# Requesting the first sixteen value pages of the sample group's stick-breaking stage one stage earlier

## The reference, cut to what matters

```python
z = jnp.einsum('bqhd,blhd->bhql', q, k).astype(jnp.float32) * (D_HEAD ** -0.5)
log_beta = jax.nn.log_sigmoid(z)
log_keep = jnp.where(mask, log_beta - z, 0.0)
after = lax.cumsum(log_keep, axis=3, reverse=True) - log_keep
w = jnp.where(mask, jnp.exp(log_beta + after), 0.0)
return jnp.einsum('bhql,blhd->bqhd', w.astype(v.dtype), v)
```

## Time and profile before

| | us |
|---|---|
| median of 3 runs | 4935.95 |
| lowest and highest run | 4934.9, 4941.7 |
| span of the profiled execution, first to last instruction | 4937.4 |
| index stage's key requests by SP | 978.2 to 987.6 |
| stick-breaking stage, first instruction to last score cap | 988.6 to 1363.0 |

### The profile page before, as it was taken

One profiled execution on the slowest core, in us unless ns is written; L12 is line 12 of the kernel. 1 busy time (PEld: TensorE's weight loads), 2 busy tenths in 40 slices (PEclk: granted clock), 3 DMA queues, 4 the chain that ended last, 5 costly groups with the idle time before them and its releaser, 6 DMA issues. The chain is left out here.

```text
span 4937.4 us, 82552 instructions
## 1 busy us (share of the span) xinstructions
PE 4283.9 (87%) x33016; PEld 3158.5 (64%) x33016; DVE 2783.5 (56%) x3905; ACT 1081.8 (22%) x1979; POOL 319.0 (6%) x443
## 2 busy tenths in 40 slices
PE   8997989877767789999996999688886969999997
PEld 5565335444434478887993655377784548888896
DVE  4798665289921355555335122479986155555444
ACT  1200554344431112222001011122222012222100
POOL 0000000400054000000000000122220000000000
PEclk9998999899978899999997999799997979999998
DMA  3012000399965211112442231422213211111343
GB/s 101 22 39 64 1 1 1 89 345 348 363 192 155 70 34 42 42 42 59 118 118 90 70 111 65 156 62 56 62 34 154 73 63 39 40 42 52 103 116 119
DMA packets 539511, 463.29 MB, mean 94 GB/s; under 512 B 77602, under 2 KB 453962, under 8 KB 534747
## 3 DMA queue, kind: packets, MB, share of 16 engines
q1 hardware_dynamic: 508386, 409.36, 26.2%
q10 hardware_dynamic: 21088, 32.80, 2.0%
q0 software_dynamic: 9728, 16.80, 1.2%
HBM read 397.01 MB, written 61.71 MB: 93 GB/s over the span
## 5 line engine op out<-in xcount | busy, mean ns | idle before, releaser
L313 PE MATMUL proj_acc<-hT,oT 128*128 128x352 f32 x864 | 258.4, 462 | 6.2 <-SPq L287 6.2
L2440 PE MATMUL fdown_acc<-hidden,oT 128*128 128x176 f32 x1584 | 248.3, 316 | 0.0
L2440 PEld LDWEIGHTS fdown_acc<-hidden,oT 128*128 128x128 f32 x1584 | 242.8, 193 | 0.7 <-issue 0.5
L313 PEld LDWEIGHTS proj_acc<-hT,oT 128*128 128x128 f32 x864 | 165.4, 192 | 99.5 <-SPq L287 7.1
L2184 PE MATMUL fup_acc_a<-h,w_up_first 128*128 128x264 f32 x704 | 169.7, 396 | 50.8 <-ACTq L2217 50.8
L2184 PEld LDWEIGHTS fup_acc_a<-h,w_up_first 128*128 128x128 f32 x704 | 137.5, 196 | 77.4 <-ACTq L2217 52.9
L517 DVE TENSOR_SCALAR_CACHE_REDUCE oT<-scores,proj_cand 128x384 bf16<-128x384 f32 (+1 forms) x186 | 164.4, 943 | 1.1
L2184 PE MATMUL fup_acc_c<-h,oT 128*128 128x264 f32 x704 | 163.8, 386 | 0.0
L2184 PE MATMUL fup_acc_d<-oT 128*128 128x264 f32 x704 | 163.8, 386 | 0.0
L2184 PE MATMUL fup_acc_b<-oT 128*128 128x264 f32 x704 | 163.8, 386 | 0.0
L2184 PE MATMUL fup_acc_d<-h,oT 128*128 128x264 f32 x704 | 163.8, 386 | 0.0
(11 more groups left out here) (645 smaller groups left out, 8608.0 us busy)
## 6 DMA issues: line engine op xcount, KB each, us to landing
oT<-in_ffn_w_down SPq DMA_DIRECT2D x96, 704.0 KB, 4.5
fup_w<-in_ffn_w_up SPq DMA_DIRECT2D x66, 512.0 KB, 4.9
scores<-in_cache_sb_k SPq DMA_DIRECT2D x128, 256.0 KB, 5.8
qb<-in_cache_sb_k SPq DMA_DIRECT2D x128, 256.0 KB, 6.2
qi<-in_cache_sb_v SPq DMA_DIRECT2D x128, 256.0 KB, 5.8
ka<-in_cache_sb_v SPq DMA_DIRECT2D x128, 256.0 KB, 6.3
w_up_first<-in_ffn_w_up SPq DMA_DIRECT2D x22, 512.0 KB, 3.8
x_between<-oT SPq DMA_DIRECT2D x16, 528.0 KB, 2.7
```

Source lines behind the costliest of these rows:

```text
L313: last = pe.matmul(acc[u][0:m, c, 0:CW], w[u][:, k, 0:m], hT[:, k, c * CW:(c + 1) * CW], start=(k == 0), stop=(k == KD - 1))
L2440: last = pe.matmul(bank[n], weights[:, k, :], moving[:, k, :], start=begin and k == 0, stop=k == DOWN_K - 1, skip_group_check=True)
```

## The change

Value pages 0 to 15 are requested by SP in the index stage, right behind the sixteen key pages (`ask_step_values`), into the same ring slots as before. Their sixteen semaphores are therefore allocated before that stage. In the loop of the stick-breaking stage, iteration t no longer requests value page t but value page t + 8, from page 16 on; the wait of each request on the page it overwrites is unchanged.

```diff
+def step_value_slot(A, i):
+    return half_columns(A.qi, i) if i < STEP_PAGES // 2 else half_columns(A.ka, i - STEP_PAGES // 2)
+
+def ask_step_values(nc, eng, K, A, I, arrived):
+    vc = I.cache_sb_v[0].rearrange("n p h d -> n p (h d)")
+    for t0 in range(0, STEP_PAGES, 8):
+        numbers = page_numbers(nc, eng, K.pages_steps[0], 4 * NPG - 8 - t0, 8, vc.shape[0])
+        for i, number in enumerate(numbers):
+            eng.dma_start(step_value_slot(A, t0 + i), vc[bass.ds(number, 1)].rearrange("o p n -> p (o n)")).then_inc(arrived[t0 + i], 16)
...
-        k_in, next_in = K.step_keys_in, K.unit_keys_in
-        s.sems += k_in
-        v_in = [s.sem(f"v_in{i}") for i in range(VR)]
+        k_in, v_in, next_in = K.step_keys_in, K.step_values_in, K.unit_keys_in
+        s.sems += k_in + v_in
...
             for t in range(n_pages):
                 if t + KR < n_pages:
                     load_k(t + KR)
-                load_v(t)
+                if VR <= t + PP < n_pages:
+                    load_v(t + PP)
             ask_unit_keys(nc, sp, K, A, I, next_in)
...
             ask_step_keys(nc, sp, K, A, I, own, K.step_keys_in)
+            ask_step_values(nc, sp, K, A, I, K.step_values_in)
...
+            K.step_values_in = [nc.alloc_semaphore(f"step_values_in{i}") for i in range(STEP_PAGES)]
```

## The result

The changed kernel takes 5074.01 us (median of 4 runs, 5071.06 to 5081.21) against 4937.56 (4 runs, 4934.9 to 4941.7): 2.8% slower, ratio 1.0278 with a 95% interval of 1.0265 to 1.029. The forecast was 5008 with a range of 4975 to 5045. Sign and place were right, and the size was too small: 136 us instead of 72.

The account below looks back on a forecast made before the run. DVE's 11.20 us per paged step was taken as the bound. The 4937.4 us span plus 9.4 for the index stage and 62.6 for the loop, less 1.45, gave 5008 us, range 4975 to 5045.

Parts of the forecast that it names:

- The count of 26 steps: Stick-breaking loop: keys of steps 3 to 15 and 19 to 31 come late, 26 times; steps 16 to 18 keep their lead.
- Part 1: End of the index stage: sixteen added value requests on SP delay the next stage's start by 9.4 us, covered by nothing.
- The sentence that the early values buy nothing: First value use in the stick-breaking stage: no wait for value pages exists today, so requesting them earlier gains 0.
- part 2: Stick-breaking loop: value requests eight iterations earlier hold back keys on SP, 2.5 us more per step, 62.6 us in all.
- last turn: PE in each late step: from the last key page's landing through its transposes, 0.7 us (0.5 to 1.2).
- values to release: Each late step: from PE's first value matmul to SP's released value request, 1.2 us (1.2 to 1.8).
- request to first landing: Each late step: the released request lands in 2.7 us, the view's minimum, as the queue is empty.
- 13 pages more: Each late step: from first landing to the batch's last key page, 13 x 0.70 = 9.1 us (8.8 to 9.6).
- loop: Stick-breaking stage: one circle of values, release, landings and turn lasts 13.7 us, against DVE's 11.2 us per step.
- The keys in time: Turn in each paged iteration: keys land early enough, DVE's 11.2 us stays, only the later start remains; 4945 us, chance 5%.
- the shorter loop: Stick-breaking loop: key requests overlap the earlier batch's tail, so a step is 12.4 us; 4974 us in all, chance 13%.
- The longer loop: Stick-breaking loop: PE pauses and a lower clock stretch its work, 15.3 us a step; 5051 us in all, chance 16%.

Follow-up runs that it names:

- e8: The changed kernel, but the loop's value pages from 16 on are requested by POOL with the same waits, SP keeping the keys alone: 4948.49 us, ratio 1.0016.
- e2: The changed kernel without early requests in the index stage; SP requests value pages 0 to 7 ahead of the loop, page t + 8 in iteration t: 5066.2 us.
- e1: The changed kernel with the sixteen early requests kept, but the loop requests value page t in iteration t, as before the change: 4949.25 us, ratio 1.0019.
- p1: A kernel with no computation: SP alone loads pages in bursts of 16 or 32; the fifteen pages after the first take 11.0 to 12.2 us.
- e4: The changed kernel with value requests six iterations ahead instead of eight: 4997.45 us, ratio 1.012.
- e5: The changed kernel, but PE does the transposes of each step's first seven key pages twice, to the same place: 5061.76 us, ratio 1.0255.

## Why the prediction was right or wrong

**The place and the mechanism were right.** Keys held behind a value request that waits for its buffer: e8 keeps the wait, moves it off SP, and the loss is gone; e2 has the loop's order alone and has the loss. The count of 26 steps, with steps 16 to 18 spared, is what the caps show.

**Part 1 was right.** 9.4 us predicted; 9.6 for the two blocks in the trace, 8.9 in e1's median. The sentence that the early values buy nothing held: e1's stage, 374.1 us to the last cap, is not shorter than the 374.4 before by more than 0.3. The advice of the Trainium skill ("DMA: Bandwidth & Descriptors", section "Rules for kernel authors") to issue a transfer early and wait on it late, weighed there, thus gives nothing here (e1, +8.9 us). In e2 the requests that were moved earlier cost 131 us, because they stand, waiting, ahead of others.

**The step that failed is the loop's length in part 2,** "1.2 + 2.7 + 9.1 + 0.7 = 13.7 us". Term by term, each a median of the 24 late steps (the medians need not add up; the last turn is counted to the end of its transposes, as in the prediction, and the next values start 0.07 us before that):

| Term | Predicted (bounds) | Measured |
|---|---|---|
| values to release | 1.2 (1.2 to 1.8) | 2.08 |
| request to first landing | 2.7 | 2.71 |
| 13 pages more | 9.1 (8.8 to 9.6) | 10.38 |
| last turn | 0.7 (0.5 to 1.2) | 1.16 |
| loop | 13.7 (to 15.3) | 16.19 |

Two causes were left out. The release and the 13 pages came out above their bounds, the last turn just inside. The 1.3 us in the 13 pages are the start of an empty queue: I priced the first page by the minimum of the earlier trace rows, which held, and the 13 behind it at nearly the full rate of the earlier trace rows, which was read where the queue keeps running. p1 shows about 1.4 us for such a start by itself, and e4 shows that a page inside the batch costs 0.68, near the 0.70 that I had. The trace of before already held one: with all earlier pages landed, the page requested at 1212.45 landed after 2.70 us and the 13th page after it 9.98 us later, above the bound of 9.6. The 0.9 and 0.5 us in release and turn are the clock: with PE's pauses the granted clock fell to 0.73, where I took durations from a stage at 0.94. e4's rows at either level and e5, which brings both back to about 1.2 and 0.7, show it.

The durations show the clock's part when the groups of one line are put side by side (groups by line and form, over the stretch between the first and the last paged cap: busy, mean ns of one, idle before; first the kernel before, then the changed one).

```profile
L1078 PE MATMUL sstick_o<-ka,sstick_wT 128*32 128x512 f32 x240 | 30.1, 619 | 0.0
```

```profile
L1092 PE MATMUL sstick_o<-ka,sstick_wT 128*32 128x512 f32 x240 | 45.6, 903 | 0.0
```

The same 240 matmuls take 903 ns instead of 619 each.

With 5.0 us per step instead of 2.5, 26 steps make 128.4 us instead of 62.6, and this difference of 66 is the size of the whole miss (5074 against 5008). That it fits so well is in part luck: in the profiled execution the later start cost 3 us more than the 9.4, and the rest of the program took 9 less.

**The rivals.** The keys in time (4945) fell by the caps. So did the shorter loop (4974): nothing of the start is hidden, and before each late step's release all earlier pages have landed. The longer loop (5051, 16%) was the nearest and named the clock, but with 15.3 us it was too short as well, and its chance too low: what I put against it, that "the work per step is unchanged, and only pauses grow", was no argument: the lower clock came with the pauses, and went when e5 filled them.

## What to carry to other kernels

A request that is moved ahead of its buffer's release holds back every request behind it on the same in-order engine; before moving it, write down which request then stands behind the wait and when that one is needed. If a circle results, price it as one: each turn pays the start of an empty queue (here 2.7 us for the first page and about 1.4 more within the next), and the engine that pauses in it may run its own steps at the lower clock. Durations read in a stage where queue and engine are busy are the wrong price for both.

## What the hardware showed that was not expected

PE was busy for 76% of the stretch before, at a granted clock of 0.94, and for 77% of it after, at 0.73, a mix of the levels of 2.4 and 1.2 GHz; what was new is its waits for pages, 97.8 us in 155 waits of at most 2.5 us. With lead six it was 0.88. Transposes without use, put into those waits, brought it to 0.98 and the last cap 20.8 us forward.

A transfer queue that starts empty doesn't reach its rate with the first landing: in p1 each start lost about 1.4 us behind it, in the burst shown with a microsecond at 180 GB/s.

Requests issued by POOL beside SP's stretched eight of SP's from 3.95 to 8.57 us, and the next stage began only 0.43 us after the last landing.
